# Gate products from raw turned tokens, and a new order of VectorE's work, in a one-core hybrid encoder layer

## The reference

```python
h = _rmsnorm(h_res, mix_norm[l])
u = h @ w_in[l]
u_conv, q_a, k_a, v_a, q_h, f_h, i_h, g_h = _split_cols(u)
y_conv = _conformer_conv(u_conv, conv_dw_w[l], conv_dw_b[l], conv_ln_g[l], conv_ln_b[l])
y_attn = _swa_mixer(q_a, k_a, v_a, attn_sinks[l])
y_hgrn = _hgrn2_mixer(q_h, f_h, i_h, g_h, lbs[l], hgrn_norm_g[l])
h_res = h_res + jnp.concatenate([y_conv, y_attn, y_hgrn], axis=-1) @ w_out[l]
h_res = h_res + _hier_moe(_rmsnorm(h_res, ffn_norm[l]), ...)
return _rmsnorm(h_res, final_norm)[:, N_META:]
```

## Time and profile before

| | us |
|---|---|
| median of 3 runs | 520.67 (519.86 to 522.13) |
| the profiled execution | 522.48 |
| its span, first to last instruction | 520.7 |
| TensorE busy | 487.0 (94%) |
| VectorE busy | 281.9 (54%) |
| ScalarE busy | 154.7 (30%) |
| GpSimd busy | 48.5 (9%) |
| chain that ended last, TensorE's share | 73% |
| chain that ended last, DMA's share | 14% |

### The profile page before, as it was taken

How to read it: one execution, slowest core, us unless ns; L and a number is a source line. 1 busy time by engine, 2 the same in 40 slices (tenths; PEclk the granted TensorE clock), 3 DMA queues, 4 the chain that set the end, 5 groups by cost and what they waited for, 6 DMA issues and landing times.

```text
span 520.7 us, 11035 instructions
## 1 busy us (share of the span) xinstructions
PE 487.0 (94%) x4521; PEld 326.3 (63%) x4521; DVE 281.9 (54%) x693; ACT 154.7 (30%) x386; POOL 48.5 (9%) x58
## 2 busy tenths in 40 slices
PE   5999999999998899999989999999999999975794
PEld 4888889888785445457565565666556555543441
DVE  3787998899768845526367332333244222232266
ACT  5420257410344423422034322222122121111134
POOL 3410000000001000000110111211201211000000
PEclk9999999999998899998999999999999999998799
DMA  8990000000009799517688899999999999999984
GB/s 279 356 373 34 0 2 0 1 1 1 3 3 354 259 431 397 227 42 299 244 286 312 353 417 335 401 427 420 426 420 423 421 421 427 418 427 426 416 344 164
DMA packets 29459, 143.04 MB, mean 275 GB/s; under 512 B 4669, under 2 KB 12022, under 8 KB 20704
## 3 DMA queue, kind: packets, MB, share of 16 engines
q1 hardware_dynamic: 23360, 131.03, 63.4%
q0 software_dynamic: 5760, 10.89, 6.0%
q10 hardware_dynamic: 288, 0.39, 0.2%
HBM read 133.73 MB, written 17.30 MB: 290 GB/s over the span
## 4 chain that ended last, share of the span: by engine, by line
PE 73%; DMA 14%; DVE 8%; issue 2%; ACT 1%; SPq 1%; POOL 1%; DVEq 0%; POOLq 0%
PE bank_pair L1534 12%; PE bank_pair L1736 11%; PE bank_pair L1876 11%; DMA area_x<-in_w_exp 8%; PE bank_pair L1884 6%; PE bank_pair L1899 5%; PE bank_pair L1544 4%; DMA area_g<-expert_out 3%; PE bank_pair L1907 3%; PE bank_pair L1474 3%; PE bank_pair L1869 3%; PE bank_pair L1678 2%; DMA expert_out<-area_m,cst 2%; DVE area_m L932 2%; PE bank_pair L1752 1%
## 5 line engine op out<-in xcount | busy, mean ns | idle before, releaser
L1736 PE MATMUL bank_pair<-area_w,area_m 128*128 128x512 f32 x128 | 60.0, 623 | 0.4 <-issue 0.4
L1736 PEld LDWEIGHTS bank_pair<-area_w,area_m 128*128 128x128 f32 x128 | 24.8, 199 | 29.1 <-issue 29.1
L932 DVE SCALAR_TENSOR_TENSOR area_m<-area_g,cols,area_m 128x512 f32<-128x512 f32 x60 | 41.4, 745 | 0.0
L1876 PE MATMUL bank_pair<-area_w,area_m 128*64 128x256 f32 x320 | 38.5, 383 | 1.2 <-ACT area_m L1988 1.2
L1876 PEld LDWEIGHTS bank_pair<-area_w,area_m 128*64 128x64 f32 x320 | 22.2, 137 | 15.5 <-issue 4.0
L1876 PE MATMUL bank_pair<-area_g,area_m 128*64 128x256 f32 x256 | 31.1, 385 | 0.0
L2103 DVE COPY cst<-bank_pair 128x128 f32<-128x128 f32 (+1 forms) x38 | 9.9, 261 | 31.2 <-PE bank_pair L1890 22.5
L2112 DVE TENSOR_TENSOR cst<-cst,bank_pair 64x128 f32<-64x128 f32 x20 | 5.9, 293 | 37.6 <-ACT cst L2026 33.9
L2121 DVE COPY area_m<-bank_pair 64x512 f32<-64x512 f32 x20 | 13.9, 693 | 21.9 <-PE bank_pair L1899 21.9
L1884 PE MATMUL bank_pair<-area_w,area_m 128*32 128x128 f32 x576 | 21.1, 291 | 4.1 <-DMA area_w<-in_w_exp 4.1
L1884 PE MATMUL bank_pair<-area_g,area_m 128*32 128x128 f32 x640 | 22.9, 286 | 1.8 <-DMA area_g<-in_w_exp 1.4
(11 more groups left out here) (448 smaller groups left out, 903.7 us busy)
## 6 DMA issues: line engine op xcount, KB each, us to landing
area_g<-in_w_exp SPq DMA_DIRECT2D x14, 2048.0 KB, 27.2
area_w<-in_w_exp SPq DMA_DIRECT2D x13, 2048.0 KB, 18.4
area_w<-in_w_exp SPq DMA_DIRECT2D x16, 1024.0 KB, 23.0
area_g<-in_w_exp SPq DMA_DIRECT2D x14, 1024.0 KB, 25.9
area_x<-in_w_exp SPq DMA_DIRECT2D x4, 2048.0 KB
area_w<-in_w_in SPq DMA_DIRECT2D x7, 1024.0 KB, 14.7
area_w<-in_w_out SPq DMA_DIRECT2D x2, 2048.0 KB, 17.0
expert_out<-area_g SPq DMA_DIRECT2D x2, 2048.0 KB, 23.4
```

Of the source, the lines that this page charges most:

```text
L932: ins = V.scalar_tensor_tensor(out=mixT[:, i, :], in0=src, scalar=w, in1=mixT[:, i, :], op0=ALU.mult, op1=ALU.add)
L1736: ins = T.matmul(bank[7][:, :], mixT[:, k, j * P:(j + 1) * P], w_out_sb[:, n, k, :], start=(k == 0), stop=(k == KT - 1))
L1876: ins = T.matmul(out_b[h * BC:(h + 1) * BC, 0:2 * P], x[:, k, :], w_gate_up[slot][:, :, k, h * P:(h + 1) * P], start=(k == 0), stop=(k == ...
```

## The change

- The host now also hands over the tokens already turned (`turned`: per partition the eight feature tiles of 528 raw tokens, in `area_x` as `raw`) and the small parameters as columns (`params`). The loads of the token rows, of the meta tokens and of the parameter rows are gone, and so are the transposes and the copies that follow them.
- The gates are products of raw tokens with gate weights that VectorE has multiplied by `mix_norm`; they run tile by tile in step with four token loads and three loads of gate weights. VectorE multiplies them by the factor 1/root of each token (`root`) afterwards, and then comes the sigmoid.
- The sums of squares: ScalarE squares the eight tiles, VectorE adds them up, a product with ones sums over the partitions and spreads the result (after the sixth tile of the gates), and ScalarE makes `root`. VectorE then writes `hT` as raw times `mix_norm` times `root`.
- TensorE makes the keys directly behind the gates, and no longer behind "hf". Three fill matmuls on a zeroed tile stand ahead of the gates.
- VectorE makes the weight sums of "a" in GpSimd's place, and all weight sums lie nearer to their use. The taps by stage are 3 in "hq", 6 in "hf", 3 behind it, 4 in "hg" (with `qb` among them), 8 in "q0", 5 and 2 behind it.
- ScalarE makes all key copies: those of attention right after the keys, and all of `k2` and `k2m`.
- Two more parts of "q1" stand ahead of the loop, and only P4 in it; the filter's means come in after step 1, its squares after step 4, its factor after step 8.

The core of the diff:

```diff
-        SQUARES_AT = 3
-        NORM_AT = 6
-        PARTS_AT = (9, 10, 11)
-        ADD_AT = (10, 11, 12)
+        MEANS_AT = 1
+        SQUARES_AT = 4
+        NORM_AT = 8
+        LAST_PART_AT = 10
+        ADD_AT = (5, 11)
...
-        LOADS = [(C_GATE, 256), (C_A, 256), (C_HQ, 256), (C_HF, 256), (C_HG, 256), (C_Q, 512), (C_K, 256), (C_HI, 256)]
-        LOAD_OF = {"gate": 0, "a": 1, "hq": 2, "hf": 3, "hg": 4, "q": 5, "k": 6, "v": 7}
-        EVAC = PROD
+        LOADS = [(C_A, 256), (C_K, 256), (C_HQ, 256), (C_HF, 256), (C_HG, 256), (C_Q, 512), (C_HI, 256)]
+        LOAD_OF = {"a": 0, "k": 1, "hq": 2, "hf": 3, "hg": 4, "q": 5, "v": 6}
+        GATE_KS = (slice(0, 2), slice(2, 4), slice(4, 8))
+        EVAC = ["k", "gate0", "gate1", *PROD[3:]]
...
+            gate_in(0)
+            raw_in(0)
+            gate_in(1)
+            raw_in(1)
+            gate_in(2)
+            raw_in(2)
+            raw_in(3)
...
+            act.dma_start(cols[:, :], params).then_inc(d_par, 16)
             act.dma_start(cst[:, 0:K_FIRST], table[:, 0:K_FIRST]).then_inc(d_cst, 16)
             act.preload_act_table_set("natural_log_exp_and_others")
+            for k in range(KT):
+                act.wait_ge(d_x[k // 2], 16)
+                nc.scalar.activation(hT[:, k, :], raw[:, k, :], ACT.Square).then_inc(squared, 1)
             act.wait_ge(d_cst, 16)
-            def first_norm(j):
-                rws = META if j == NT else P
-                src = meta_x[:, :] if j == NT else xs[:, j, :]
-                act.wait_ge(d_meta if j == NT else d_x[j], 16)
-                junk = area_g[0:rws, 2 * (TAPS - 1 + TT):2 * (TAPS - 1 + TT) + D]
-                step(nc.scalar.activation(junk, src, ACT.Square, accum_out=ss[0:rws, j:j + 1]))
-                step(nc.scalar.activation(rstd[0:rws, j:j + 1], ss[0:rws, j:j + 1], ACT.Ln, bias=eps[0:rws], scale=1.0 / D))
-                nc.scalar.activation(rstd[0:rws, j:j + 1], rstd[0:rws, j:j + 1], ACT.Exp, scale=-0.5).then_inc(rstd_ready, 1)
-                act.wait_ge(rstd_ready, NORMS.index(j) + 1)
-
-            def turned_out(h):
-                act.wait_ge(xT_done, 2 * h + 2)
-                for k in (2, 3, 6, 7):
-                    nc.scalar.activation(hT_pair(h, k), turned_pair(h, k), ACT.Copy, scale=cols[:, 62 + k:63 + k]).then_inc(hT_a, 1)
-
-            for j in NORMS[0:3]:
-                first_norm(j)
-            act.wait_ge(cols_ready, 1)
-            turned_out(0)
-            for j in NORMS[3:]:
-                first_norm(j)
-            turned_out(1)
+            act.wait_ge(ss_done, 1)
+            for h in range(2):
+                step(nc.scalar.activation(root[:, half_cols(h)], bank[4 + h][:, 0:HALF], ACT.Ln, bias=eps, scale=1.0 / D))
+            nc.scalar.activation(root, root, ACT.Exp, scale=-0.5).then_inc(root_ready, 1)
+            act.preload_act_table_set("sigmoid_and_others")
...
+            act.wait_ge(product, made("k"))
+            keys_out(0)
+            first_copy("a")
...
+            keys_out(1)
             for i in range(2):
-                n = f"gate{i}"
-                act.wait_ge(product, made(n))
-                nc.scalar.activation(sig[:, i, 0:HALF], half_of(n, 0), ACT.Sigmoid).then_inc(a_step, 1); an[0] += 1
-                nc.scalar.activation(sig[:, i, HALF:], half_of(n, 1), ACT.Sigmoid).then_inc(evac, 1)
+                act.wait_ge(hT_v, KT + 5 + 2 * (i + 1))
+                nc.scalar.activation(sig[:, i, :], sig[:, i, :], ACT.Sigmoid).then_inc(evac, 1)
...
+            V.memset(warm, 0.0).then_inc(warm_ready, 1)
...
+            def gate_weights(i):
+                dve.wait_ge(d_gate[i], 16)
+                for k in range(GATE_KS[i].start, GATE_KS[i].stop):
+                    w = w_in_sb[:, k, C_GATE:C_GATE + 256]
+                    V.tensor_scalar(w, w, cols[:, 62 + k:63 + k], None, ALU.mult).then_inc(gate_w, 1)
+
+            def square_added(k):
+                dve.wait_ge(squared, k + 1)
+                if k >= 2:
+                    dve.wait_ge(sq_added, k - 1)
+                V.tensor_tensor(hT[:, 0, :], hT[:, 0, :], hT[:, k, :], ALU.add).then_inc(sq_added, 1)
...
+            dve.wait_ge(d_par, 16)
+            gate_weights(0)
+            gate_weights(1)
+            square_added(1)
+            square_added(2)
+            gate_weights(2)
+            for k in range(3, KT):
+                square_added(k)
+            weight_sums("a")
+            dve.wait_ge(root_ready, 1)
+            for k in range(KT):
+                V.scalar_tensor_tensor(out=hT[:, k, :], in0=raw[:, k, :], scalar=cols[:, 62 + k:63 + k], in1=root,
+                                       op0=ALU.mult, op1=ALU.mult).then_inc(hT_v, 1)
+
+            dve.wait_ge(product, made("gate1"))
+            dve.wait_ge(hT_v, KT)
+            lo, hi = slice(0, KH), slice(KH, KT)
+            V.tensor_tensor(tw1, hT[:, lo, EDGE:], hT[:, lo, META:EDGE], ALU.subtract).then_inc(hT_v, 1)
+            V.tensor_copy(tw2[:, :, 0:META], hT[:, lo, 0:META]).then_inc(hT_v, 1)
+            dve.wait_ge(hT_v, KT + 1)
+            V.tensor_tensor(tw2[:, :, META:], hT[:, hi, EDGE:], tw1, ALU.subtract).then_inc(hT_v, 1)
+            V.tensor_tensor(tw3, hT[:, hi, EDGE:], hT[:, lo, EDGE:], ALU.subtract).then_inc(hT_v, 1)
+            dve.wait_ge(hT_v, KT + 3)
+            V.tensor_tensor(tw4, hT[:, hi, 0:EDGE], tw2, ALU.subtract).then_inc(hT_v, 1)
+            for i in range(2):
+                for h in range(2):
+                    V.tensor_tensor(sig[:, i, half_cols(h)], half_of(f"gate{i}", h), root[:, half_cols(h)], ALU.mult).then_inc(hT_v, 1)
+            weight_sums("hq", range(1))
...
-            for n, taps in (("hq", (0, 0, 2, 1, 1)), ("hf", (2, 1, 2, 1, 1))):
-                for o in range(5):
-                    conv(taps[o])
-                    add_part(n, o)
-            conv(2)
+            for o in range(5):
+                weight_sums("q0" if o else "hg", (range(1, 4), range(0, 2), range(2, 4), (), ())[o])
+                conv((0, 0, 1, 1, 1)[o])
+                add_part("hq", o)
+            for o in range(5):
+                weight_sums("q1", (range(0, 3), range(3, 4), (), (), ())[o])
+                conv((1, 1, 2, 1, 1)[o])
+                add_part("hf", o)
+            conv(3)
...
+            for o, taps in enumerate((0, 1, 1, 1, 1)):
                 conv(taps)
+                if o == C22:
+                    mark(V.tensor_tensor(qb, qf, eb, ALU.mult))
...
-                    V.tensor_copy(k2[hp * HD:hp * HD + HD, 1::2, ti, :], src[HD:P, :, hp, :]).then_inc(k2_v, 1)
...
-            for o, taps in enumerate((0, 1, 2, 1, 1)):
+            for o, taps in enumerate((3, 1, 2, 1, 1)):
                 conv(taps)
                 add_part("q0", o)
+            conv(5)
+            add_part("q1", U2)
             conv(TAPS - tap[0])
-            add_part("q1", U2)
+            add_part("q1", S15)
...
-            add_part("q1", S15)
-            dve.wait_ge(conv_means, 1)
-            for i in range(2):
-                V.tensor_tensor(mixT[:, i, :], mixT[:, i, :], bank[7][:, :], ALU.subtract).then_inc(cen_done, 1)
-
+            add_part("q1", C22)
...
+            pe.wait_ge(warm_ready, 1)
+            for _ in range(3):
+                T.matmul(bank[7][:, 0:2 * P], warm[:, 0:P], warm[:, P:3 * P], start=True, stop=True)
+            for k in range(KT):
+                pe.wait_ge(d_x[k // 2], 16)
+                pe.wait_ge(gate_w, k + 1)
+                for i in range(2):
+                    n = f"gate{i}"
+                    for h in range(2):
+                        ins = T.matmul(half_of(n, h), w_in_sb[:, k, COL[n]:COL[n] + P], raw[:, k, half_cols(h)],
+                                       start=(k == 0), stop=(k == KT - 1))
+                    if k == KT - 1:
+                        ins.then_inc(product, 1)
+                if k == KT - 3:
+                    pe.wait_ge(d_cst, 16)
+                    pe.wait_ge(sq_added, KT - 1)
+                    for h in range(2):
+                        ins = T.matmul(bank[4 + h][:, 0:HALF], cst[:, K_ONE:K_ONE + P], hT[:, 0, half_cols(h)], start=True, stop=True)
+                    ins.then_inc(ss_done, 1)
+
+            pe.wait_ge(d_win[LOAD_OF["k"]], 16)
+            for k in range(KT):
+                pe.wait_ge(hT_v, k + 1)
+                for h, t in enumerate((slice(0, cut_of("k")), slice(cut_of("k"), TT))):
+                    ins = T.matmul(half_of("k", h), w_in_sb[:, k, C_K:C_K + P], hT[:, k, t], start=(k == 0), stop=(k == KT - 1))
+            ins.then_inc(product, 1)
...
-            fill(bank[1], 4)
-            turn_tile(0)
-            pe.wait_ge(d_par, 112)
-            T.transpose(bank[6][:, 0:86], rows[:, :], ident[0:86, 0:86]).then_inc(small_T, 1)
-            turn_tile(1)
-            pe.wait_ge(xn_ready, NORMS.index(NT) + 1)
-            for k in range(KT):
```

(21 more changed lines are left out.)

238 lines of the change are left out of this document (86 added, 152 removed).

## The result

| | before | after |
|---|---|---|
| median, same chip | 520.52 (4 runs) | **512.63** (4 runs) |
| ratio, 95% interval | | 0.9849 [0.9814, 0.9883] |
| profiled execution, its span | 522.48, 520.7 | 512.79, 511.0 |
| TensorE busy | 487.0 | 480.5 |
| VectorE busy | 281.9 | 287.8 |

The forecast was 513.1 us. One of the four executions of the changed kernel ran in a slower state (522.03 us at a mean granted clock of 0.958); the ratios and intervals of this document leave such executions out (one here, one in e0_after, three in e6_k2_on_vector, two in e7_old_taps), the medians keep them.

What follows compares the result with a forecast made beforehand. The prediction took TensorE as the bound up to 160 us, with VectorE close behind. Gains of 6.7 + 0.5 + 0.4 = 7.6 us, taken from the median 520.67, gave 513.1 us, range 510.0 to 517.6 us.

Steps and rivals of the forecast that it cites:

- The opening: From the start to the values: gates from 5.7 to 23.4 us, keys behind them, "a" at 30.5 us; gain 6.7 us.
- rival A: In the opening: the clock is up at once, 2.6 us more gain, 510.5 us; chance 0.15.
- The keys as cover: Behind the gates: keys cost their 7.12 us while VectorE stays ahead, so "a" waits for nothing.
- VectorE from 31 us on: VectorE's order up to "q1": level stage from 71.3 us to about 95 us, S15 of "q1" out at about 126.2 us.
- slack of 0.3 us: At P3 of "q1", the tightest place: S15 out at about 126.2 us, TensorE there at 126.5 us.
- rival B: VectorE becomes the bound, TensorE stalls at P3 of "q1" and for C22: gain 3.6 us, 517.1 us; chance 0.18.
- The loop: In "q1": the 0.52 us stall before step 2 goes (+0.5 us), two parts fewer in the loop (+0.4 us).
- behind it nothing is changed: After the loop's end at 149.5 us: no change, except output projection loads 9 us earlier and the router's 8 us.
- Rival C: In the experts: the gain does not reach the end, as the weight stream ends where it ended; 520.7 us; chance 0.06.
- Rival D: In the opening: the clock stays down, through all of gates and keys at worst, 532.8 us; chance 0.05.

Runs made afterwards that it cites:

- e0_after: The changed kernel run again, unaltered: 514.78 us, ratio 0.988.
- e6_k2_on_vector: The changed kernel with four copies of turned keys and the two meta-token copies back on VectorE: 520.52 us, ratio 0.9949.
- e7_old_taps: The changed kernel with the filter's 31 taps put back into the stages where they were before: 521.5 us, ratio 0.9989.
- f2_after_again: The changed kernel run once more, unaltered, as partner of the late loads: 511.44 us, ratio 0.9842.
- e3_late_loads: The changed kernel with SyncE waiting for the third unit of scores before loading residual rows and output weights: 511.23 us, ratio 0.9823.
- e5_keys_late: The changed kernel with the keys back behind "hf" and ScalarE's key copies behind the exponential of `kf`: 521.38 us, ratio 1.0018.
- f3_p3_in_loop: The changed kernel with part P3 of "q1" behind step 2 of the loop instead of ahead of the loop: 513.33 us (1 run).

## Why the prediction was right

- **The opening** (6.7 us): gates from 5.7 to 23.4 us foretold, 5.80 to 23.48 found; "a" at 30.5 and 30.60; values at 67.6 and 67.72. The first landing (0.80 MB at 5.7 us) was right within 0.1 us, the second (1.61 MB, foretold for 8.1 us) was 1.3 us late:

```profile
9.45 1.18 ACT L592 ACTIVATE area_h<-area_x 128x528 f32<-128x528 f32 x2 [2.49 <-DMA area_x<-in_turned]
```

At the lower clock TensorE had not reached it, so it cost nothing here. The choice of the clock's rise at 10.9 us (10.78 found) was right for this execution and no more than that: nine traces of this opening lie between 4.1 and 10.8 us, and rival A's case, the clock up when the gates start, came true in two of them (4.61 in f2_after_again, 4.14 in e3_late_loads). It gave 2.2 us (keys at 21.27 us), not the 2.6 of the rival, since the gates then wait 0.3 to 0.4 us for that second pair. My value and rival A's were the two ends of a range that one and the same kernel runs through.
- **The keys as cover**: the sum said that they cost their 7.12 us and that VectorE stays ahead under them. e5_keys_late shows the price without it, 5.5 us.
- **VectorE from 31 us on**: level stage at 71.3 "or half a microsecond later", found 72.24, 0.4 us later than even that (six instructions of taps behind "hf" took 4.05 us and ended at 72.2); it ended at 95.3 us, foretold 95. "hg" 90.5 and 90.64, S15 of "q1" 126.2 and 126.58, P3 126.5 and 126.99 us. The slack of 0.3 us was 0.4, and e6_k2_on_vector shows that it was all there was: rival B was a near thing, and its mechanism decides from 0.4 us of extra work on.
- **The loop** (0.5 + 0.4 us): no wait before step 2, and the part in the loop costs 1.92 us (1.93 in the earlier trace rows). From the start of the values to the loop's end it took 82.05 us, where before took 82.94 (74.19 to 157.13): 0.89 us, the two terms together. f3_p3_in_loop, with one of the two parts moved back, gives 0.3 us for the wait and 0.2 us for a part, as the sum had them, less 0.2 us that come back elsewhere. The loop ended at 149.77 us, 149.5 foretold; the gain there is 7.36 us in place of 7.6. What is missing lies in the opening: I took 74.35 us for the values' start from the chain of waits, where TensorE's own order of time has 74.19, and the changed kernel had 67.72 in place of 67.6.
- **The step that failed** is "behind it nothing is changed". From the loop's end to the first expert load it took 2.4 us more: the fetch that meets the loads. The cause stood in the sum's next clause, that the loads for the output projection start earlier (8.4 us, 9 foretold); I put its price at nothing. The first expert load came at 172.08, not 169.5 us. It did not show in the total of the profiled executions, since the profiled execution of before met the lower clock twice behind 177 us and after did not (3.4 us), so their 9.7 us are 7.4 - 2.4 + 3.4 and 1.3 us of later differences whose cause is open. So the total agrees with the sum in part by luck: the gain at the loop's end less the stand is 5.0 us. In f2_after_again, with the clock up early, the first load came at 169.13 us. By the medians of the three comparisons the gain was 7.9, 4.5 and 8.3 us, mean 6.9, a little under the forecast of 7.6.
- **Rival C** fell: the gain at the second expert load, 6.7 us, is 8.9 us at 413 us and 9.7 us at the end; less the clock's 1.7 and 3.4 us it is 5.0, 5.5 and 6.3 us. **Rival D** fell: no wait for a raw pair stood between the gates, and where one of 0.4 us did (f2_after_again) the clock stayed up. The rule of the Trainium skill on clock drops between bursts ("HAM oscillation — how this bites in real kernels") says that waits for DMA between bursts of matmuls send the clock down again; in the opening it found no wait to act on. A fall behind a wait is seen where I did not look for it: behind the 3.82 us wait for VectorE in e5_keys_late, where the granted clock was 0.58.

## What to carry to other kernels

Where two engines run at 97% side by side, the order of the second one's work is worth as much as the work: the same 31 taps in other stages cost 5.8 us more. A step that can run early is worth moving to where another engine's chain would leave the bound engine idle, since it covers that chain. A bulk load that is started earlier can meet an instruction fetch; a wait of TensorE for "issue" with the DMA engines full is its mark, and here it went when the loads were issued some 6.5 us later.
